# Half of the early weight remainders made by GpSimd instead of VectorE

## The reference

```
mod = silu(c) @ w_ada + b_ada
shift, scale, gate = split(mod, 3)
h = rms(x, norm_g) * (1 + scale) + shift
proj = h @ w_in            # 2048 x 8192
# attention and a gated recurrence over proj, then @ w_out, then the second block
```

## Time and profile before

| | |
|---|---|
| median of 3 runs | 2609.45 us |
| span of the profiled execution | 2608.5 us |
| TensorE busy | 2581.8 us, 99% |
| VectorE busy | 1030.5 us, 40% |
| ScalarE busy | 1081.2 us, 41% |
| GpSimd busy | 1139.6 us, 44% |

### The profile page before, as it was taken

One profiled execution on the slowest core, in us unless ns is written; L12 is line 12 of the kernel. 1 busy time (PEld: TensorE's weight loads), 2 busy tenths in 40 slices (PEclk: granted clock), 3 DMA queues, 4 the chain that ended last, 5 costly groups with the idle time before them and its releaser, 6 DMA issues.

```text
span 2608.5 us, 33094 instructions
## 1 busy us (share of the span) xinstructions
PE 2581.8 (99%) x13414; PEld 2076.9 (80%) x13414; DVE 1030.5 (40%) x1622; ACT 1081.2 (41%) x1769; POOL 1139.6 (44%) x580
## 2 busy tenths in 40 slices
PE   8989999999999999999999999999999999999999
PEld 3668777877888888878888888888888888888887
DVE  3774444434344431244685433334333223312300
ACT  4334434444444532344444444444444444333311
POOL 0004434434434454543454444445555556554543
DMA  9863333223333234422222323323333333333443
GB/s 399 313 227 106 114 106 105 90 97 114 114 117 113 85 124 145 134 89 81 89 81 85 106 97 102 108 84 111 113 105 115 113 112 117 114 111 115 146 145 104
DMA packets 97784, 322.84 MB, mean 124 GB/s; under 512 B 10976, under 2 KB 13024, under 8 KB 93024
## 3 DMA queue, kind: packets, MB, share of 16 engines
q1 hardware_dynamic: 92016, 301.16, 33.8%
q10 hardware_dynamic: 5616, 19.56, 2.0%
HBM read 303.90 MB, written 16.78 MB: 123 GB/s over the span
## 4 chain that ended last, share of the span: by engine, by line
PE 96%; DVE 3%; DMA 0%; ACT 0%; issue 0%; POOL 0%; SPq 0%; DVEq 0%; ACTq 0%
PE bank L822 28%; PE bank L824 28%; PE bank L823 28%; PE bank L765 2%; PE bank L1017 1%; PE bank L1006 1%; DVE TA L1608 1%; PE bank L937 1%; PE bank L1000 1%; DVE first L1608 1%; PE bank L971 1%; DVE wlo L1591 1%; PE bank L1053 0%; PE bank L1068 0%; PE bank L864 0%; PE bank L1044 0%
## 5 line engine op out<-in xcount | busy, mean ns | idle before, releaser
L2123 POOL TENSOR_TENSOR wlo<-wraw,whi 128x1024 fp32r<-128x1024 f32 (+3 forms) x420 | 970.0, 2310 | 1331.3 <-ACT whi L1123 1331.2
L822 PE MATMUL bank<-Hhi,whi 128*128 128x512 f32 x2720 | 1093.6, 402 | 0.2 <-POOL Hlo L2227 0.2
L824 PE MATMUL bank<-Hhi,wlo 128*128 128x512 f32 x2720 | 1061.9, 390 | 0.0
L823 PE MATMUL bank<-Hlo,whi 128*128 128x512 f32 x2720 | 1060.5, 390 | 0.0
L1123 ACT ACTIVATE whi<-wraw 128x1024 fp32r<-128x1024 f32 (+3 forms) x438 | 440.3, 1006 | 663.5 <-PE bank L824 647.2
L822 PEld LDWEIGHTS bank<-Hhi,whi 128*128 128x128 f32 x2720 | 510.9, 188 | 113.8 <-issue 9.9
L824 PEld LDWEIGHTS bank<-Hhi,wlo 128*128 128x128 f32 x2720 | 510.5, 188 | 109.3
L823 PEld LDWEIGHTS bank<-Hlo,whi 128*128 128x128 f32 x2720 | 511.3, 188 | 103.8 <-issue 2.2
L822 PE MATMUL bank<-Ohi,whi 128*128 128x512 f32 x320 | 127.9, 400 | 0.0
L824 PE MATMUL bank<-Ohi,wlo 128*128 128x512 f32 x320 | 124.8, 390 | 0.0
L823 PE MATMUL bank<-Olo,whi 128*128 128x512 f32 x320 | 124.6, 389 | 0.0
(11 more groups left out here) (272 smaller groups left out, 2734.5 us busy)
## 6 DMA issues: line engine op xcount, KB each, us to landing
wraw<-in_w_in SPq DMA_DIRECT2D x293, 512.0 KB, 3.5
TA<-in_w_ada SPq DMA_DIRECT2D x22, 1024.0 KB, 11.0
first<-in_w_ada SPq DMA_DIRECT2D x32, 512.0 KB, 4.4
wraw<-in_w_out SPq DMA_DIRECT2D x32, 512.0 KB, 3.5
wraw<-in_w_o SPq DMA_DIRECT2D x32, 512.0 KB, 3.5
first<-in_w_ada SPq DMA_DIRECT2D x10, 1024.0 KB, 7.8
wmem<-in_w_mem ACTq DMA_DIRECT2D x16, 512.0 KB, 9.2
wraw<-in_w_beg ACTq DMA_DIRECT2D x16, 512.0 KB, 6.7
```

The lines of the kernel that those rows point to most:

```text
L822: e.matmul(out, hi[:, c], xhi[k], start=first and j == 0, stop=False)
L823: e.matmul(out, hi[:, c], xlo[k], start=False, stop=False)
L824: m = e.matmul(out, lo[:, c], xhi[k], start=False, stop=last and end)
L2123: e.tensor_tensor(M.wlo[b][:, 0:w], M.wraw[b][:, 0:w], M.whi[b][:, 0:w].bitcast(F32), ALU.subtract).then_inc(S.lo)
```

## The change

GpSimd makes the remainders of pieces 4, 6, 8, 10, 12, 14 and 16. It makes piece k + 1 in its `h(k)`, so for k = 3, 5, ..., 15. VectorE leaves these seven out and keeps pieces 0 to 3, 5, 7, ..., 17. So that `lo` still counts in order, each remainder that follows one of the other engine waits for it.

```diff
+RESTS_BY_POOL = range(4, FIRST_RESTS, 2)
...
     def rest_of(j):
-        if j < FIRST_RESTS:
+        if j < FIRST_RESTS and j not in RESTS_BY_POOL:
             b, w = j % NRING, ITEMS[j][3]
+            if j - 1 in RESTS_BY_POOL:
+                dve.wait_ge(S.lo, j)
             dve.wait_ge(S.hi, j + 1)
...
     def remainder(j):
-        if FIRST_RESTS <= j < len(ITEMS):
+        if j in RESTS_BY_POOL or FIRST_RESTS <= j < len(ITEMS):
             b, w = j % NRING, ITEMS[j][3]
-            pool.wait_ge(S.lo, FIRST_RESTS)
+            pool.wait_ge(S.lo, j if j < FIRST_RESTS else FIRST_RESTS)
             pool.wait_ge(S.hi, j + 1)
             e.tensor_tensor(M.wlo[b][:, 0:w], M.wraw[b][:, 0:w], M.whi[b][:, 0:w].bitcast(F32),
                             ALU.subtract).then_inc(S.lo)

     def h(k):
         n.up("phi")
+        if k:
+            remainder(k + 1)
```

## The result

The changed kernel takes 2622.72 us (median of 5 runs, 2620.42 to 2623.02) against 2609.45 (5 runs, 2608.87 to 2609.59): 13.3 us or 0.51% slower; the ratio over all runs is 1.0049, with a 95% interval of 1.0038 to 1.006. The profiled execution has a span of 2621.4 us, 12.9 more than before. The forecast was 2620.0, the range 2615.5 to 2623.5.

What follows compares the result with a forecast made beforehand. VectorE's chain was taken to bound blocks 5 to 15, TensorE everything behind. Five pairs at 9.4 us plus 1.05 for piece 6 gave + 10.5 us, a median of 2620.0 us, range 2615.5 to 2623.5.

Steps and rivals of the forecast that it cites:

- The bound, and what passes to the end: VectorE bounds blocks 5 to 15, TensorE the rest; any change up to block 15 shifts everything behind one for one.
- What the removal gives: In VectorE's chain, a removed remainder gives 0.19 us a block, not 1.13, because `Hlo` then waits for `Hhi`.
- What the addition costs: Pieces 8 to 16: GpSimd waits for `ada`, then delays the scaling by 2.07 us; net + 1.88 a pair, 9.4 us.
- Piece 6: GpSimd's remainder runs into `Hlo` of tile 5, partly hidden in the wait for `Hhi`: + 1.05 us.
- piece 4: GpSimd's remainder delays `Hlo` of tile 3 at no cost, with 0.9 us of cover.
- the added waits: VectorE's waits for `lo` and ScalarE's transfers waiting for GpSimd's remainders cost nothing.
- The sum of the chain: Pieces 8 to 16 and piece 6 together lengthen VectorE's chain up to block 15: 9.4 + 1.05 = 10.5 us.
- The clock: Rival: TensorE falls to a lower rate behind 3.6 us gaps, only block 15 pays, + 2.65, 2622.6 us; chance 0.11.
- VectorE first: Rival: GpSimd gets in only while `Hlo` waits for `Hhi`; six pieces at 1.05, 6.3 us, 2615.8 us; chance 0.08.
- No contention: Rival: GpSimd doesn't hold up VectorE's `ada` and scaling; only - 1.1 us remains, 2608.3 us; chance 0.08.
- The full gain: Rival: `Hhi` is not late and there is no contention in VectorE's chain; - 6.8 us, 2602.7 us; chance 0.03.

Runs made afterwards that it cites:

- the addition alone: Kernel before, VectorE keeping all remainders, plus GpSimd subtracting two halves of a constant at the same seven moments, with nothing waiting for it: 2624.41 us.
- the removal alone: Changed kernel with GpSimd making only one column of each of the seven early remainders, the other 1023 left out: 2607.99 us.
- the `ada` ahead: Kernel before, all remainders on VectorE, with three ada moved into earlier blocks where VectorE waits for ScalarE: 2603.23 us, ratio 0.9974.
- the products with zeros: Changed kernel plus eight TensorE products with zeros behind each of blocks 6, 8, 10, 12 and 14: 2619.20 us.
- the run with GpSimd's copies: Kernel before plus GpSimd copying 128x1024 of a constant, one SBUF input, at the seven moments: 2614.42 us, ratio 1.002.

## Why the prediction was right, and where it was not

**The bound, and what passes to the end.** Right. Behind block 15 the two kernels are equal to 0.2 us in 2425.

**What the removal gives.** Right: 0.19 forecast, 0.20 a block measured (6.98 or 6.99 for 7.19). The step that mattered was to ask what `Hlo` waits for next, and to price it by tile 0.

**What the addition costs.** Right in mechanism and place. Scaling + 2.01 where + 2.07 was forecast; a pair + 1.8 (+ 1.88). One case went otherwise: the high part of piece 10 came only at 132.6, because TensorE, slow in block 7, released its buffer late. GpSimd then came behind the scaling and held the second `ada`, for a pair of + 1.95. That is within the term's bounds, but its cause, TensorE's clock, was not in the sum. The Trainium skill, Advanced Engine Details and Errata, section VectorE Performance Modes, names only VectorE's two-port modes as the ones that interfere; a scaling of 2.76 us, float32 with two SBUF inputs, shows that this is too narrow. The Trainium skill, GPSIMD Engine Reference, section 1. Specifications, which counts two SBUF inputs in, fits.

**Piece 6, piece 4, the added waits.** + 1.05 forecast, + 1.02 measured (98.30 to 106.51 against 7.19); nothing and nothing, and the run with pieces 4 and 6 alone says so by itself. No row shows VectorE or a transfer waiting for GpSimd's count.

**The sum of the chain.** 10.5 forecast, 10.27 at the start of block 15. The prediction's "77.0 us hold 11 such blocks" is a slip (11 blocks of 7.19 us are 79.1); nothing in the sum hangs on it.

**The clock.** This is what the forecast had wrong. It was a rival with a chance of 0.11 and the sum went without it, so the measured time lies outside the sum's own bounds (2618.5 to 2621.5) and inside the range only because that was drawn wide enough for this rival. In the profile it came, and the priced 2.65 us (from rows 10) were 2.75: block 15 at 8.31 for 5.56 us. Its outcome, 2622.6, is the measured 2622.7. That the price fits so well is partly luck: in three other profiles the fall before block 15 cost 1.6. Two matmul rows of the kernel after, behind a gap of 3.29 us, 0.43 apart (1.2 GHz), where rows at 2.4 GHz are 0.23 apart:

```profile
187.97 0.76 PE L787 MATMUL bank<-whi,Hhi 128*128 128x512 f32 x1 [3.29 <-DVE Hlo L1629]
...
188.96 0.63 PE L789 MATMUL bank<-wlo,Hhi 128*128 128x512 f32 x1
189.39 0.63 PE L787 MATMUL bank<-whi,Hhi 128*128 128x512 f32 x1
```

Also right was that only block 15 pays: the chain is 109.28 us with falls in blocks 7, 9 and 11 and with falls in 11 and 13. What failed is the weight: a granted clock of 1.00 with gaps of 1.5 us was read as evidence for gaps twice as long, although rows 10 showed what an idle TensorE does, and the change itself made the gaps longer. The Trainium skill, TensorE: Matmul & The Clock Gate, section HAM oscillation, describes a fall behind each of a row of such waits; the trace agrees in part, with falls behind the gaps of 3.30, 3.48 and 3.29 us and of 2.32, and none behind the one of 3.27 before block 13.

**The rivals.** VectorE first (2615.8) is out by the scaling's 2.76 us. No contention (2608.3) is out by the addition alone, and is what the removal alone gives. The full gain (2602.7) is out, and is nearly what the same removal gives where `Hhi` isn't late (4.5 of 2603.2 to 2598.7, in four blocks).

## What to carry to other kernels

Before moving work from a full engine to an idle one, ask two things of the rows: what the next instruction waits for once the work is gone, and whether the two engines can run beside each other at all. Here the first left 0.2 of 1.1 us and the second took 2.0. And when a change lengthens the gaps of an engine whose clock depends on its work, price the block behind the last gap at the low clock; if work must be moved, look first for idle time of the same engine, as the `ada` ahead did for 6.6 us.

## What the runs showed of the hardware

- A GpSimd copy with one SBUF input shuts out VectorE's two-input instructions for its own 0.90 us just as a subtraction does for 2.26.
- The length of a gap alone doesn't decide whether TensorE's clock falls. It fell behind gaps of 1.30 and 1.60 us (with the products with zeros before them) and of 2.16 and 2.73. In the run with GpSimd's copies it stayed at 2.4 GHz in block 7 and fell in block 15, both behind 2.16 us. In the changed kernel it stayed up behind one of 3.27:

```profile
171.79 0.47 PE L787 MATMUL bank<-whi,Hhi 128*128 128x512 f32 x1 [3.27 <-DVE Hlo L1629]
172.09 0.40 PE L788 MATMUL bank<-whi,Hlo 128*128 128x512 f32 x1
```

- The clock can fall after TensorE has begun to work again. In the run with GpSimd's copies the second and third matmul of block 15 start 0.23 apart, the third and fourth 0.40:

```profile
181.42 0.41 PE L788 MATMUL bank<-whi,Hlo 128*128 128x512 f32 x1
181.65 0.60 PE L789 MATMUL bank<-wlo,Hhi 128*128 128x512 f32 x1
182.05 0.63 PE L787 MATMUL bank<-whi,Hhi 128*128 128x512 f32 x1
```

- A fall cost block 15 2.75 us in one profile and 1.6 in three others (7.13 to 7.15 for 5.56). What decides between these stays open, and so does when the clock falls.
